# Half output projection under the last pairs of heads: chunks added to the residual in their own slot, weight split moved to the last slot

## What is computed

```
s = einsum('bnqhgd,bnkhd->bhgqk', q, kb) * 64**-0.5
s = where(mask, s + bias, NEG);  m = maximum(max(s), sink)
p = exp(s - m);  p = p / (sum(p) + exp(sink - m))
o = einsum('bnhgqk,bnkhd->bnqhgd', p, vb)
return o.reshape(B, T, 1024) @ w_out          # added to the residual h
...
h = h + square(relu(rmsnorm(h) @ w_up)) @ w_down
```

## Time and profile before

| | |
|---|---|
| median of 3 runs | 2232.43 us (2232.38 to 2233.07) |
| profiled execution, its own time | 2213.66 us |
| its span, first to last instruction | 2211.9 us |
| mean granted TensorE clock | 0.974 |
| TensorE busy with matmuls | 2075.8 us, 94% of the span |
| VectorE busy | 992.8 us, 45% |
| ScalarE busy | 740.2 us, 33% |
| the slots of the sliding-window attention with their fills | about 1698 to 1817 us of the span |
| SOB's eight chunks | 1818.76 to 1841.17 us |
| MLP3 | from 1841.17 us |

### The profile page before, as it was taken

How to read it: one execution, slowest core, us unless ns; L and a number is a source line. 1 busy time by engine, 2 the same in 40 slices (tenths; PEclk the granted TensorE clock), 3 DMA queues, 4 the chain that set the end, 5 groups by cost and what they waited for, 6 DMA issues and landing times.

```text
span 2211.9 us, 29302 instructions
## 1 busy us (share of the span) xinstructions
PE 2075.8 (94%) x12936; PEld 1677.3 (76%) x12936; DVE 992.8 (45%) x1256; ACT 740.2 (33%) x1078; POOL 116.2 (5%) x99
## 2 busy tenths in 40 slices
PE   7998688889989999999989899999999989999997
PEld 5865477769778888887787788888887668888886
DVE  4365355356445423434644554324335745423433
ACT  3132433254234322333322333213323634312321
POOL 3144000000000000001000000000000310000000
PEclk9999699989989999999999999999999999999999
DMA  6211000025262232322322022232223212232221
GB/s 217 78 57 58 1 3 3 3 77 161 88 84 89 94 99 91 96 95 78 96 77 76 20 77 96 95 95 95 95 95 96 58 44 90 95 95 95 96 76 38
DMA packets 163710, 175.59 MB, mean 79 GB/s; under 512 B 4245, under 2 KB 157861, under 8 KB 163456
## 3 DMA queue, kind: packets, MB, share of 16 engines
q1 hardware_dynamic: 161600, 166.74, 23.5%
q0 software_dynamic: 1984, 6.98, 2.0%
HBM read 168.47 MB, written 5.24 MB: 79 GB/s over the span
## 4 chain that ended last, share of the span: by engine, by line
PE 89%; DVE 5%; ACT 4%; issue 1%; DMA 1%; SPq 0%; DVEq 0%; ACTq 0%
PE M L1107 24%; PE M L1109 24%; PE M L1108 24%; PE X L464 2%; PE M L1155 1%; PE M L1156 1%; PE M L1157 1%; PE M L464 1%; ACT mt L512 1%; PE M L1350 1%; PE X L1338 1%; PE X L1235 1%; PE X L777 1%; DMA h<-in_x_dram 1%; PE X L1216 1%
## 5 line engine op out<-in xcount | busy, mean ns | idle before, releaser
L1642 DVE TENSOR_TENSOR w_lo<-raw,w_hi 128x2048 fp32r<-128x2048 f32 x155 | 354.2, 2285 | 360.6 <-ACT w_hi L1406 360.6
L1406 ACT ACTIVATE w_hi<-raw 128x2048 fp32r<-128x2048 f32 x155 | 293.7, 1896 | 422.1 <-PE M L1109 369.9
L1107 PE MATMUL M<-f,w_hi 128*128 128x512 f32 x768 | 304.2, 396 | 0.0
L1108 PE MATMUL M<-f,w_lo 128*128 128x512 f32 x768 | 303.0, 395 | 0.0
L1109 PE MATMUL M<-u,w_hi 128*128 128x512 f32 x768 | 303.0, 395 | 0.0
L1107 PE MATMUL M<-u,w_hi 128*128 128x512 f32 x768 | 303.0, 395 | 0.0
L1108 PE MATMUL M<-u,w_lo 128*128 128x512 f32 x768 | 303.0, 395 | 0.0
L1109 PE MATMUL M<-f,w_hi 128*128 128x512 f32 x768 | 303.0, 395 | 0.0
L1108 PEld LDWEIGHTS M<-f,w_lo 128*128 128x128 f32 x768 | 144.7, 188 | 34.5 <-issue 0.7
L1107 PEld LDWEIGHTS M<-f,w_hi 128*128 128x128 f32 x768 | 144.7, 188 | 34.3 <-issue 0.7
L1108 PEld LDWEIGHTS M<-u,w_lo 128*128 128x128 f32 x768 | 144.7, 188 | 33.8
(11 more groups left out here) (477 smaller groups left out, 3306.0 us busy)
## 6 DMA issues: line engine op xcount, KB each, us to landing
raw<-in_w_up_dram SPq DMA_DIRECT2D x48, 1024.0 KB, 5.4
raw<-in_w_down_dram SPq DMA_DIRECT2D x48, 1024.0 KB, 5.1
raw<-in_w_in_dram SPq DMA_DIRECT2D x13, 1024.0 KB, 5.4
raw<-in_a_w_in_dram SPq DMA_DIRECT2D x12, 1024.0 KB, 5.3
raw<-in_w_out_dram SPq DMA_DIRECT2D x4, 1024.0 KB, 5.3
raw<-in_w_mk_dram SPq DMA_DIRECT2D x4, 1024.0 KB, 5.2
raw<-in_w_mv_dram SPq DMA_DIRECT2D x4, 1024.0 KB, 5.2
raw<-in_w_mq_dram SPq DMA_DIRECT2D x4, 1024.0 KB, 5.2
```

What stands on the lines that cost most here:

```text
L1107: mm(dst, wh, xh, start=start, stop=False)
L1108: mm(dst, wl, xh, start=False, stop=False)
L1406: nc.scalar.activation(w_hi[:, n % 2, :, 0:cols], raw[:, n % 4, :, 0:cols], ACT.Copy).then_inc(S["w_hi_ready"], 1)
L1642: TTO(w_lo[:, n % 2, :, 0:cols], raw[:, n % 4, :, 0:cols], w_hi[:, n % 2, :, 0:cols].bitcast(f32), ALU.subtract).then_inc(S["w_lo_ready"], 1)
```

## The change

Three edits. The split of block SOB moves from slot 6 to slot 7 (`HI_SW`, on ScalarE and on VectorE). VectorE's adds of SOA's chunks are written in the slot in which TensorE makes them, but for the last of each slot, and behind the place of the split. And TensorE no longer waits for all eight `sw_lo` before SOB's chunk 0, but for one more of them before each of its four parts.

```
+        HI_SW = {-2: N_WQ + 2, 0: N_WQ + 3, 2: N_SOA, 4: N_SOA + 1, 7: N_SOB}
...
@@ tensor
-            wait("sw_lo", KT)
-            for b in range(2):
-                for c in range(4):
-                    chunk_part(N_SOB + b, c, s_hi, s_lo, 0, 1, at=4, flat=True)
+            for part in range(4):
+                wait("sw_lo", 5 + part)
+                chunk_part(N_SOB, 0, s_hi, s_lo, part, 4, at=4, flat=True)
+            for c in range(1, 8):
+                chunk_part(N_SOB + c // 4, c % 4, s_hi, s_lo, 0, 1, at=4, flat=True)
@@ scalar
-                if c % 2 == 0:
-                    hi(N_WQ + 3 + c // 2)
+                if c in HI_SW:
+                    hi(HI_SW[c])
@@ vector
-                for j in FILL_SOA.get(c - 1, ()):
-                    resid_chunk(N_SOA, 0, j)
+                if c - 1 in FILL_SOA:
+                    resid_chunk(N_SOA, 0, FILL_SOA[c - 1][-1])
...
-                if c % 2 == 0:
-                    lo(N_WQ + 3 + c // 2)
-            for j in FILL_SOA[KT - 1]:
-                resid_chunk(N_SOA, 0, j)
+                if c in HI_SW:
+                    lo(HI_SW[c])
+                for j in FILL_SOA.get(c, ())[:-1]:
+                    resid_chunk(N_SOA, 0, j)
+            resid_chunk(N_SOA, 0, FILL_SOA[KT - 1][-1])
```

## The result

| | before | after |
|---|---|---|
| median of 6 runs | 2227.86 us (2215.98 to 2233.07) | 2211.73 us (2207.24 to 2213.17) |
| profiled execution | 2213.66 us | 2207.24 us |

The ratio is 0.9935, with a 95% interval of 0.9909 to 0.9961: faster, by 8.7 to 20.3 us. The predicted time of 2224.1 us is 12.4 us too high, and 2211.73 us lies outside the range. The two profiled executions differ by 6.4 us only. So three numbers have to be brought together: 8.3 us worked out, 6.4 us between the profiles, 16 us between the medians.

The account below looks back on a forecast made before the run. TensorE was taken to bound the kernel, so time lay in its waits and low clock. 5.18 us pause + 1.64 us clock + 1.51 us before SOB = 8.33 us; 2232.43 - 8.33 = 2224.1 us, range 2222.0 to 2227.5 us.

Parts of the forecast that it names:

- the base: Whole kernel: median of runs shown, 2232.43 us, is 18.8 us above the profiled execution, taken as same for both kernels.
- the sum: Slots 6 and 7 to SOB: 5.18 + 1.64 + 1.51 = 8.33 us gained, giving 2224.1 us.
- The ring: Slot 6: chunk 4 waits for an add behind SOB's remainder, which waits for ScalarE's rounded part, which waits for chunk 3; 5.0 us.
- 6.82 us for slot 6: Slot 6 against slot 7: gain from moving the split, 5.18 us pause plus 1.64 us clock (0 to 3.0 us).
- 1.51 us at the end: Before SOB's chunk 0: four-part waits let nine matmuls cover the wait for pair 7, gaining 1.51 us.
- The adds at zero: VectorE's adds of SOA: writing them in their own slot moves them past nothing by itself, so zero gain.
- The spare time at chunk 7, 0.31 us: Slot 7: rounded part to freed bank takes 5.48 us, TensorE takes 5.79 us to chunk 7, leaving 0.31 us.
- Downstream, up to 0.5 us lost: At MLP3, TensorE arrives 8.3 us earlier; if VectorE's norm steps move only 6.8 us, 0.5 us is lost.
- Slower: Rival at MLP3: the later load of the block four behind SOB comes too late; about 2237 us, chance 0.03.
- The clock did not fall all the same: Rival in slots 6 and 7: pause goes but small gaps keep the 3.3 us slow stretch; 2225.7 us, chance 0.09.
- The ring did not close in slot 7: Rival at chunk 7: a late add brings back a 5.0 us pause with slow clock; 2230.9 us, chance 0.05.
- Nothing was lost further on: Rival: saved time lost at a later wait, likeliest the norm before MLP3; whole, 2232.4 us, chance 0.04.

Follow-up runs that it names:

- the sets: Three later rounds of timing, kernels taking turns with the kernel before on one chip; the kernel before ran 32, 23 and 17 times: 2220.84, 2220.41, 2221.35 us.
- adds alone: Kernel before with only the adds written in their own slot, so same instructions in the same order: 2220.83 against 2220.84 us, ratio 1.0004.
- first set: First round of later timing; the changed kernel, without further edit, took 2213.87 us against 2220.84 us for the kernel before.
- second and third sets: Later rounds of timing; the changed kernel, without further edit, took 2212.49 against 2220.41 us and 2211.69 against 2221.35 us for the kernel before.

## Why the prediction was wrong, step by step

**The step that failed** is the base to which the sum was applied: "The median of the runs shown is 18.8 us above the profiled execution; I take that difference as the same for both kernels". It wasn't. In the sets the median of a kernel lies anywhere from 10.4 us below its own profiled execution (adds alone) to 5.3 us above it (changed kernel, first set), and for the changed kernel of the second and third sets 1.3 and 1.2 us below. The three runs shown agreed within 0.7 us, and I read that as how sure the number was. The kernel's own median is 2220.4 to 2221.4 us by 72 executions. 8.3 us less than that is about 2212.5 us, and the changed kernel has 2211.7 to 2213.9 us. So the 18.8 us were no property of the kernel before that the changed one shares: by those medians the distance would have been 6.7 to 7.7 us. There was a sign: one program, two numbers 18.8 us apart, and 8.3 us to be told. The range allowed for the change's own uncertainty and for next to nothing in the base. That the clock moves a whole execution by 17 us is shown with the adds-alone kernel; that it also made the first three slow is argued from this, since their clock isn't listed. Why those three were alike stays open, and so does whether the chip that they ran on had a part in it, since it isn't listed either.

**The ring** chunk 3, rounded part, remainder, add, chunk 4 was right. It is broken by moving the split (12.71 us), and nearly as well by moving one add (13.24 us), and it comes back one slot later when the split stands one place further back (19.46 us).

**6.82 us for slot 6**: 19.52 - 12.70 = 6.82 us between the two profiles. In it, the 5.18 us of pause repeat to a hundredth in the three profiles that have it. The clock's part was given as 0 to 3.0 us with 1.64 us taken. These three have 1.64, 1.94 and 2.14 us, and the moved pause 2.78 us. The range was right, the value some tenths low.

**1.51 us at the end**: 2.86 - 1.35 = 1.51 us, as it was; SOB itself then takes 1834.71 - 1812.22 = 22.49 us instead of 22.41, so 1.43 us of it are left at MLP3. **The adds at zero**: 1.0004. **The spare time at chunk 7, 0.31 us**: 0.31 us. **Downstream, up to 0.5 us lost**: nothing, MLP3 begins 8.24 us earlier, when slot 6 is taken as the start, and from there to the end both profiles take 370.7 us. The load that moved is that of MLP3's third block, which ScalarE took up at 1855.31, and not of its second, as the rival "Slower" has it.

**The sum** of 8.33 us: the three sets have 7.0, 7.9 and 9.7 us between the medians, 8.2 us on average, and 0.9956 to 0.9961 as ratios. The first comparison's interval of 8.7 to 20.3 us just misses it; half of its executions of the kernel before are the three slow ones.

**The rivals.** The clock did not fall all the same: it is 1.00 from 1780 to 1860 us, and slots 6 and 7 take 12.70 to 12.73 us in all four profiles of the changed kernel. The ring did not close in slot 7, though it was as near as said. Nothing was lost further on, and no load came late.

## What to carry to other kernels

An instruction that is ready, here an add, can cost TensorE the whole wait of what stands ahead of it in its engine's list. So look at what the engine did in the pause, and move the one instruction that is ready; here one add was worth 6.3 of the 8.3 us. Split a wait for all operands into one for each part when the parts become ready one after the other, and use the halves that are ready early to fill the last gap. And before a sum of 8 us is set against a time, ask how far executions of the unchanged kernel lie apart: three that agree may agree on the wrong value, and a large distance between them and the profiled execution is a sign of it.

## What the runs showed of the hardware

**The same pause costs a different amount of clock each time.** In slot 4 TensorE waits 2.43 or 2.44 us in every profile but the two in which the slot is filled. From the scores before it to slot 6 it then takes 18.50 us in the first profile, with the clock at 1.00 throughout, and 21.20 us in the profile of the changed kernel in the second set, at 0.84:

```profile
1766.90:1785.40 18.50, 15.95 (x116) 11.22 (x116) 15.82 (x26) 11.94 (x36) 6.65 (x4) 1.00 0.19 58
```

```profile
1769.80:1791.00 21.20, 18.76 (x116) 12.93 (x116) 15.95 (x25) 11.88 (x36) 6.65 (x4) 0.84 0.16 51
```

In the profile of before it is 19.87 us. The ten profiles with this pause fall into three groups: one at 18.50 us, four at 19.87 to 19.91 us, five at 21.20 to 21.31 us. So one pause costs 0, 1.4 or 2.7 to 2.8 us of clock beyond itself. The Trainium skill, page "TensorE: Matmul & The Clock Gate", section "What's actually happening", says that the number of matmuls at the low clock at a kernel's start varies from run to run of one kernel; these rows agree with such a variation, and show it behind a pause in the middle of a kernel.

**The clock can fall without a pause.** In the profile of the adds-alone kernel it fell while TensorE ran matmuls of 128 columns with no idle time, and stayed down for 20 us, from 1684.4 to 1704.4; in the eleven other profiles it stayed at 1.00 through the same instructions. This one fall cost 9.6 us, more than the whole change brings, and whether it comes is not in the instruction list.
